# Keys, gates and key norms ahead of the exponentials, values by head pairs, and a new order of output-projection loads in a two-layer encoder trunk

## Time and profile before

| what | us |
|---|---|
| median of 3 runs | 1164.49 (1164.35 to 1165.43) |
| profiled execution, own time | 1163.36 |
| its span, first to last instruction | 1161.6 |
| PE busy | 1133.9 (98%) |
| DVE busy | 575.1 (50%) |
| ACT busy | 442.5 (38%) |
| POOL busy | 119.2 (10%) |

### The profile page before, as it was taken

The page is one execution under the profiler, slowest core; times in us unless marked ns, Lnnn a source line. Parts: engine busy times, 40 slices in busy tenths (PEclk is TensorE's granted clock), DMA queues, the critical chain, the costliest instruction groups (busy, mean ns, idle before and its releaser), DMA issues.

```text
span 1161.6 us, 13614 instructions
## 1 busy us (share of the span) xinstructions
PE 1133.9 (98%) x5059; PEld 903.0 (78%) x5059; DVE 575.1 (50%) x792; ACT 442.5 (38%) x685; POOL 119.2 (10%) x154
## 2 busy tenths in 40 slices
PE   7989999999999999999999989999999999999998
PEld 5767678888888888888877754578888888888887
DVE  6578875534434433241665686565443443442221
ACT  5545444423323322231546676544332233233120
POOL 5010200001101100000204210000010010010000
PEclk9999999999999999999999998999999999999999
DMA  6522123233233233222323210023223223223231
GB/s 187 191 66 62 54 78 104 87 94 108 87 94 108 87 94 107 92 92 90 91 75 93 74 37 19 1 73 109 91 91 108 90 90 108 90 91 101 81 125 56
DMA packets 84984, 103.88 MB, mean 89 GB/s; under 512 B 10579, under 2 KB 61456, under 8 KB 84816
## 3 DMA queue, kind: packets, MB, share of 16 engines
q1 hardware_dynamic: 81792, 101.99, 28.1%
q10 hardware_dynamic: 2096, 1.05, 0.3%
q0 software_dynamic: 1056, 0.30, 0.1%
HBM read 101.23 MB, written 2.10 MB: 89 GB/s over the span
## 4 chain that ended last, share of the span: by engine, by line
PE 91%; DVE 5%; ACT 2%; DMA 1%; issue 1%; POOL 0%; ACTq 0%; DVEq 0%; POOLq 0%
PE ps L1514 28%; PE ps L1516 28%; PE ps L1515 27%; PE ps L1889 2%; PE ps L1545 2%; PE ps L1915 2%; DMA x_tok<-in_x 1%; PE ps L1904 1%; DVE e_sc L1191 1%; ACT e_sc L740 1%; DVE e_sc L1180 1%; DVE tiny L1172 1%; PE ps L1891 0%; PE ps L1625 0%; PE ps L1964 0%
## 5 line engine op out<-in xcount | busy, mean ns | idle before, releaser
L1042 DVE TENSOR_TENSOR w_lo<-raw,w_hi 128x1024 fp32r<-128x1024 f32 (+2 forms) x194 | 228.1, 1180 | 446.7 <-ACT w_hi L652 443.7
L652 ACT ACTIVATE w_hi<-raw 128x1024 fp32r<-128x1024 f32 (+2 forms) x194 | 196.1, 1017 | 489.4 <-PE ps L1516 472.8
L1514 PE MATMUL ps<-h_hi,w_hi 128*128 128x512 f32 x928 | 367.6, 396 | 0.7 <-DVE conv_h L1211 0.7
L1516 PE MATMUL ps<-h_hi,w_lo 128*128 128x512 f32 x928 | 361.6, 390 | 0.0
L1515 PE MATMUL ps<-h_lo,w_hi 128*128 128x512 f32 x928 | 361.5, 390 | 0.0
L1514 PEld LDWEIGHTS ps<-h_hi,w_hi 128*128 128x128 f32 x928 | 174.4, 188 | 42.6 <-issue 5.7
L1515 PEld LDWEIGHTS ps<-h_lo,w_hi 128*128 128x128 f32 x928 | 174.5, 188 | 38.4 <-issue 2.6
L1516 PEld LDWEIGHTS ps<-h_hi,w_lo 128*128 128x128 f32 x928 | 174.3, 188 | 36.8
L545 POOL TENSOR_TENSOR ffn_t<-ffn_t,row_scale 128x512 f32<-128x512 f32 x40 | 50.9, 1293 | 555.0 <-ACT ffn_t L817 555.0
L1514 PE MATMUL ps<-w_hi,act_hi 128*128 128x512 f32 x176 | 68.7, 390 | 0.0
L1516 PE MATMUL ps<-w_hi,act_lo 128*128 128x512 f32 x176 | 68.5, 389 | 0.0
(11 more groups left out here) (254 smaller groups left out, 1249.6 us busy)
## 6 DMA issues: line engine op xcount, KB each, us to landing
raw<-in_w_ffn_in SPq DMA_DIRECT2D x88, 512.0 KB, 3.5
raw<-in_w_ffn_out SPq DMA_DIRECT2D x44, 512.0 KB, 3.7
raw<-in_e_w_in SPq DMA_DIRECT2D x18, 512.0 KB, 3.7
raw<-in_o_w_in SPq DMA_DIRECT2D x8, 512.0 KB, 3.6
raw<-in_o_w_out SPq DMA_DIRECT2D x8, 512.0 KB, 3.5
raw<-in_e_w_out SPq DMA_DIRECT2D x8, 256.0 KB, 3.9
raw<-in_e_w_out SPq DMA_DIRECT2D x4, 512.0 KB, 4.0
out_dram<-out_tok SPq DMA_DIRECT2D x8, 256.0 KB, 3.0
```

The source lines that it names most:

```text
L652: ins = act.activation(dst, src, ACT.Copy)
L1042: ins = TT(dst, src, high, ALU.subtract)
L1514: MM(dst, st_hi, mv_hi, start=start, stop=False)
L1516: return MM(dst, st_lo, mv_hi, start=False, stop=stop)
```

## The change

1. **Key tiles.** Both loads' key tiles come first (banks 4 to 7), then the gate matmuls, then all four key means into the banks of their own keys, then the values of both loads into banks 0, 1 and 3, 4. On ACT all key norms, a root table load ahead and an exponential table load behind them, lie before the first exponential; on DVE three of the four key norms do, and the fourth is behind the maxima of head 1.
2. **Values by head pairs.** `o_pT` and a second square buffer move into the space of `h_hi`, `o_pT` is doubled, and `o_values(j)` runs the matmuls of heads 2j and 2j+1 alternately into the two halves of bank 7. `o_out(j)` copies all 128 partitions at once.
3. **yc work spread.** The gate products and the sums of squares of `yc` are done two and two around heads 0 and 1. The splits of loads 116 and 117 move from before the head loop to its end (after head 6 and after the loop).
4. **Output projections.** Both take all four loads of the early operand first (`yb`; `yc`), then all four of the late one. The mean of the late operand comes after two loads; its bank is read before the fourth output tile of the third load is written. `residual` adds tiles 0 to 3 after the sixth load. The transposes of head 7 move inside the first load of the second projection and its values behind that load's second half.

```diff
-    k_pairs = (at("k_pair_a", ..., R + 45 * K), at("k_pair_b", ..., R + 72 * K))
+    k_pairs = (at("k_pair_a", ..., R + 45 * K), at("k_pair_b", ..., h_at + 16 * K))
-    o_pT = at("o_pT", [P, 3, S], F32, R + 58 * K)
+    o_pT = at("o_pT", [P, 2, 3, S], F32, h_at)
+    k_sq = at("k_sq", [P, 2, S], F32, h_at + 12 * K)
...
# ACT
+        key_squares(0)
+        key_squares(1)
+        rms_table()
         through(111)
-        kv_tiles(0)
-        through(112)
         rms(M_OK, ps[:, 4, :], 1)
         rms(M_OK + 1, ps[:, 5, :], 1)
-        kv_tiles(1)
-        through(113)
+        value_copy(0)
+        rms(M_OK + 2, ps[:, 6, :], 1)
+        rms(M_OK + 3, ps[:, 7, :], 1)
+        exp_table()
+        value_copy(1)
...
         o_exp(0)
-        rms(M_OK + 2, ps[:, 3, :], 1)
-        rms(M_OK + 3, ps[:, 7, :], 1)
+        o_exp(1)
         for h in range(HEADS):
-            if 1 <= h < 6:
+            if 1 <= h < HEADS - 1:
                 o_exp(h + 1)
-            if h >= 1:
-                o_out(h - 1)
+            if h and h % 2 == 0:
+                o_out(h // 2 - 1)
...
+            if h == 6:
+                rms_table()
+                through(112)
+        through(113)
+        o_out(3)
...
# DVE
+        key_gains(0)
+        key_gains(1)
+        through(111)
...
         k_norm(0)
-        through(112)
-        kv_tiles(1)
+        k_norm(1)
+        value_copy(0)
+        k_norm(2)
+        value_copy(1)
...
         o_max(0)
+        yc_gate(0)
+        yc_gate(1)
         o_prob(0)
         o_max(1)
-        k_norm(1)
-        through(113)
+        yc_gate(2)
+        yc_gate(3)
+        k_norm(3)
         for h in range(HEADS):
...
+            if h < 2:
+                yc_sum(2 * h)
+                yc_sum(2 * h + 1)
...
+            if h == 6:
+                through(112)
...
+        through(113)
         yd_sum(3)
...
         def residual(rnd, out0, bank0):
-            through(out0 + 3)
-            add_x(rnd, out0 + 3, 0, bank0)
+            through(out0 + 5)
+            add_x(rnd, out0 + 5, 0, bank0)
...
# PE
         pe.wait_ge(rs_step, M_EB + 1)
-        out_group(E_OUT, 4, (yb_hi, yb_lo), (ya_hi, ya_lo), (yb_lo_ready, ya_lo_ready), ea_mean)
-        pe.wait_ge(rs_step, M_EA + 1)
-        out_group(E_OUT + 4, 0, (yb_hi, yb_lo), (ya_hi, ya_lo), (yb_lo_ready, ya_lo_ready))
+        out_loads(E_OUT, 4, (yb_hi, yb_lo), yb_lo_ready, True, ea_mean)
+        out_loads(E_OUT + 2, 0, (yb_hi, yb_lo), yb_lo_ready, True, before=ea_read)
+        out_loads(E_OUT + 4, 4, (ya_hi, ya_lo), ya_lo_ready, False)
+        out_loads(E_OUT + 6, 0, (ya_hi, ya_lo), ya_lo_ready, False)
...
             for kt in range(QT):
-                pT = (o_pT[:, 0, :], o_pT[:, 1, 0:384], o_pT[:, 2, 0:256], o_pT[:, 1, 384:512])[kt]
-                ins = MM(ps[a:a + 64, 7, P * kt:S], o_v[:, kt, 64 * h:64 * h + 64], pT,
-                         start=kt == 0, stop=kt == QT - 1)
+                for i in range(2):
+                    a, h, p = 64 * i, 2 * j + i, o_pT[:, i]
+                    pT = (p[:, 0, :], p[:, 1, 0:384], p[:, 2, 0:256], p[:, 1, 384:512])[kt]
+                    ins = MM(ps[a:a + 64, 7, P * kt:S], o_v[:, kt, 64 * h:64 * h + 64], pT,
+                             start=kt == 0, stop=kt == QT - 1)
...
+        for h in range(HEADS - 1):
+            if 0 < h:
+                if h % 2 == 0:
+                    pe.wait_ge(rs_used, used_before(M_OK + h // 2))
+                else:
+                    pe.wait_ge(ok_normed, (h + 1) // 2 + 1)
                 o_scores(h + 1)
+            if h == 2:
                 pe.wait_ge(yc_summed, 4)
                 mean(M_OC, 3, ones, acc[:, :])
+                pe.wait_ge(rs_step, M_OK + 4)
+            if h and h % 2 == 0:
+                o_values(h // 2 - 1)
+            o_turn(h)
...
         pe.wait_ge(rs_step, M_OC + 1)
+        pe.wait_ge(d_exp_done, QT * HEADS)
+        out_loads(O_OUT, 0, (yc_hi, yc_lo), yc_lo_ready, True, od_tail)
+        out_loads(O_OUT + 2, 4, (yc_hi, yc_lo), yc_lo_ready, True, before=od_read)
+        out_loads(O_OUT + 4, 0, (yd_hi, yd_lo), yd_lo_ready, False)
+        out_loads(O_OUT + 6, 4, (yd_hi, yd_lo), yd_lo_ready, False)
```

More of the change, by code:

```diff
@@ L408, in _ @@
             for j in range(2):
-                n = E_OUT + 4 * half + j
+                n = E_OUT + 2 * half + j
                 free(n)
@@ L415, in _ @@
                                  .rearrange("(k p) n -> p k n", p=64)).then_inc(raw_landed[n % 2], 16)
+        for half in range(2):
             for j in range(2):
-                wide(E_OUT + 4 * half + 2 + j, e_w_out[0], 256 * j, 512 * half, 512)
+                wide(E_OUT + 4 + 2 * half + j, e_w_out[0], 256 * j, 512 * half, 512)
         def ffn(layer):
@@ L474, in _ @@
             wide(O_UKV + j, o_w_ukv[0], 0, 512 * j, 512)
-        for half in range(2):
-            for j in range(4):
-                wide(O_OUT + 4 * half + j, o_w_out[0], 256 * j, 512 * half, 512)
+        for part in range(2):
+            for half in range(2):
+                for j in range(2):
+                    wide(O_OUT + 4 * part + 2 * half + j, o_w_out[0], 512 * part + 256 * j, 512 * half, 512)
         ffn(1)
@@ L1519, in ready, with load @@
             pe.wait_ge(lo_done, n + 1 + shift)
-        def load(n, tiles, ks, moving, banks, first, last, shift=0, extra=None):
+        def load(n, tiles, ks, moving, banks, first, last, shift=0, extra=None, before=None):
             ready(n, shift)
@@ L1532, in load @@
                 for t, b in enumerate(banks):
+                    if before:
+                        before(kk, t)
                     ins = product(ps[0:P, b, :], th[t], tl[t], mh, ml,
@@ L1660, in _, with out_loads @@
         ab(3)
[L1662 to L1669, removed]
+        def out_loads(n, b0, tiles, lo_ready, first, extra=None, before=None):
+            th, tl = tiles
+            for j in range(2):
+                pe.wait_ge(lo_ready, 2 * j + 2)
+                load(n + j, plain(512, 4), (2 * j, 2 * j + 1), lambda k: (th[:, k, :], tl[:, k, :]),
+                     range(b0, b0 + 4), first and j == 0, not first and j == 1,
+                     extra=extra and (lambda: extra(j, 0)), before=before if j == 0 else None)
                 if extra:
@@ L1864, in k_means @@
-        def k_means(half):
-            for j in range(2):
-                p = 2 * half + j
-                pe.wait_ge(ok_gained, p + 1)
-                mean(M_OK + p, K_MEAN_BANKS[p], mean64, sq[:, j, :])
+            for kk in range(2):
+                for j in range(2):
+                    ins = product(ps[:, 4 + 2 * half + j, :], keys(w_hi, kk, j), keys(w_lo, kk, j),
+                                  ckv_hi[:, kk, :], ckv_lo[:, kk, :], kk == 0, kk == 1)
+            ins.then_inc(keys_done, 1)
@@ new lines, in value_tiles @@
+        def value_tiles(half):
+            n = O_UKV + half
+            values = lambda w, kk: w[:, n % W_SLOTS, 512 * kk + 256:512 * kk + 512]
+            if half == 0:
+                pe.wait_ge(gates_ready, 2)
+            else:
+                pe.wait_ge(gates_ready, 4)
+                pe.wait_ge(rs_step, M_OK + 1)
+            for t in range(QT):
+                for kk in range(2):
+                    c = 256 * (t % 2)
+                    ins = product(ps[:, V_BANKS[half][t // 2], c:c + 256], ckv_hi[:, kk, t * P:(t + 1) * P],
+                                  ckv_lo[:, kk, t * P:(t + 1) * P], values(w_hi, kk), values(w_lo, kk),
+                                  kk == 0, kk == 1)
+            ins.then_inc(load_used, 1)
@@ L1880, in _ @@
         ins.then_inc(gates_mixed, 1)
-        k_means(0)
-        kv_load(1)
+        for p in range(4):
+            pe.wait_ge(ok_gained, p + 1)
+            mean(M_OK + p, 4 + p, mean64, k_square(p))
+        value_tiles(0)
+        value_tiles(1)
         def o_scores(h):
```

210 lines of the change are left out of this document (90 added, 120 removed).

## The result

The changed kernel takes 1155.01 us (median of 4 runs, 1154.05 to 1156.05), and the kernel before, run beside it, 1164.42 us (median of 4 runs, 1163.84 to 1165.43): ratio 0.9915, 95% interval 0.9904 to 0.9927. That is 9.4 us less. The forecast was 1157.5 with a range of 1151.5 to 1162.5. The profiled execution took 1154.55 us with a span of 1152.7, 8.9 less than the span before.

What follows compares the result with a forecast made beforehand. PE, busy 98% of the span, bounds the kernel. Terms -3.5 - 8.8 + 5.1 + 0.9 = -6.3, a second count -7.9, about the middle -7.0: median 1157.5 us, range 1151.5 to 1162.5.

Steps and rivals of the forecast that it cites:

- First projection: First output projection: 2.2 us wait for ya's sum and 1.7 us of low clock go, 0.4 guard comes: -3.5 us.
- the guard: First projection, ahead of the third load's fourth output tile: PE waits 0.4 us for DVE's norm step.
- Values by pairs: Second attention: alternate array halves run side by side, 2.4 us per head pair instead of 4.6; four pairs -8.8 us.
- New waits: Second attention: PE waits walked through four streams total 13.2 us against 8.1 before, +5.1 us.
- The small waits of 0.3 and 0.6: Second attention, after head 1's wait: PE waits for head 2's exponentials and the last sum of yc.
- the guard for the mean of `yd`: Second output projection: PE waits 0.45 us, as in the first projection.
- Low clock: Second attention: old stretch goes (-3.3), 2.5 us come after head 1's wait and 1.7 after head 7's: +0.9 net.
- two sums: Whole change: adding the terms gives -6.3 us, counting the second stage out whole gives -7.9; about the middle, -7.0, taken.
- the first: Rival: clock stays up, or waits are shorter than walked (2 us less, no low clock 4.2): 1151.5 to 1155; chance 0.17.
- The copies as a bound: Rival, head loop: DVE and ACT become the bound, handoff slips in five heads give +5, 1162.5 us; chance 0.13.
- No overlap: Rival, pair values: halves do not run side by side since both write bank 7, +8.8, 1166.3 us; chance 0.04.
- A clock that stays down through the head loop: Rival, head 1's transposes to the first load: low clock lasts between waits, about +25, 1182 us; chance 0.03.

Runs made afterwards that it cites:

- The second experiment: Changed kernel, but the matmuls of a head pair's values run one head after the other, not alternating array halves: 1160.91 us, ratio 0.9962.
- The filler: Changed kernel plus 14 matmuls of 512 columns, result unread, in PE's wait before head 7's transposes: 1152.47 us, ratio 0.9899.
- The fifth experiment: Changed kernel with load 116's split behind the head loop, and the fourth key norm and yc's sums, squares, mean and norm re-placed: 1144.78 us, ratio 0.9832.

## Why the prediction was right, point by point

- **First projection, -3.5.** Measured -3.5 (48.53 to 44.99 us); 0.1 us of idle time is left for the guard where I had 0.4. `residual` with two loads between its halves delayed nothing: no wait before a feed-forward load stands in the list. Of the 3.5 us, the low clock's part depends on the execution: with the order put back the same wait was followed by full clock, and the stage cost 2.6.
- **Values by pairs, -8.8.** Measured 4 x (4.60 - 2.31) = -9.2: the perfect bound, where I had taken 2.4 per pair. The second experiment splits it into some 3 us for two heads in different halves behind one another and 6 for alternating.
- **New waits, 13.2 against 8.1.** The step was right in its places and 3.0 us too high in its size: 122.59 - 112.37 = 10.2 us idle. Head 1: 3.3 forecast, 3.3 measured. Head 7: 4.7 and 4.5. Exponentials of head 4: 1.9 and 1.4. Exponentials of head 0: 1.4 and 0.6. For the last I had the third key norm on DVE drawn out beside POOL (up to 1.4 us a step, as the earlier trace rows show once), but POOL's product ended at 679.8 and the step took 0.74. The small waits of 0.3 and 0.6 did not come, and the guard for the mean of `yd` cost 0.1 where I had 0.45.
- **Low clock, +0.9 net.** I had 4.2 us after and 3.3 before. Measured are two stretches of 3.4 us, half of which is 3.4 in all, against 3.4 before: no change. The length is not settled by the wait: behind head 1's wait of 3.3 us the stretch is 3.4 us in the changed kernel and 6.8 with the first projection put back. The filler shows that the wait before head 7 is the cause of its stretch. The waits of the nine profiles, from the first attention on, and what stood at their end: of 14 waits of 3.0 to 4.5 us each has half clock beginning within the wait or at most 1.3 us behind it; of 15 of 2.1 to 2.5 us nine have; of those of 1.2 to 1.6 us none. The rule of the Trainium skill that I weighed (TensorE: Matmul & The Clock Gate, "HAM oscillation — how this bites in real kernels") says that bursts of matmuls broken by waits fall back to the low clock again and again, and the trace agrees for the long waits. But the waits that it tells of are of 3 to 5 us, so the third low stretch that I drew from it for a wait of 1.9 us was my reading and not the section's; the 1.4 us wait of head 4 was followed by full clock. The row that I held against it was luck in its turn: the wait of 2.4 us, harmless in the kernel before, has low clock at its end in five of the other eight profiles.
- **Sum.** -7.0 forecast, -9.4 measured by the medians. The forecast was the middle of two sums that count the second stage as -2.8 and -4.4 us; that stage measured -6.6. The difference is in the terms above: waits 3.0 too high, clock 0.9, values 0.4. (The list of new waits adds up to 13.05 and not 13.2, and the matmuls of the second sum to 107.6 and not 107.4; neither matters.) Taken off -2.8 they give -7.1, so 0.5 us stay unexplained. So the mechanism was right, and one term, the waits, was too high by 3.0 us, a third of the gain, with two smaller errors to the same side; the result lies 2.5 us below the forecast and inside the range.
- **Rivals.** Of the first, the half on shorter waits came true and the half on the clock did not; the result lies at its upper end, 1155. The copies as a bound fell by the second and fifth experiments: longer values cost nearly their full length, and the stage from the gates on runs 9.7 us faster with the same copies. (The Trainium skill, TensorEngine Tiling (Array Packing), "PSUM Bottleneck", names such a bound; these runs do not show it.) No overlap fell by the 2.31 us of a pair. A clock that stays down through the head loop did not come in any of the eight profiles with the new loop; the longest low stretch is 6.8 us.

What the change left on the table is its own wait before head 7: the split of load 116 was not moved far enough back, and it and its low clock took back 5.1 us; the order around head 1 and the norm of `yc` took another 5.1 by the medians, 4.3 by the stage.

## What to carry to other kernels

When matmuls with half-width outputs stand in one stream, alternate the two halves: 2.31 us for two heads here, 3.86 one after the other. Where streams are hand-ordered, walk each one with the durations of the old trace before moving work: work that nobody needs yet must not stand before a step that the busiest engine waits for. The fifth experiment gained by placing it where that engine has a long step. Count a long wait of TensorE (3 us and more here) at its length plus the low clock behind it: 1.6 us here before head 7, and up to twice that where the stretch was 6.8 us long. Where single executions differ by a low stretch, compare stages and not spans.

## What the runs showed of the hardware

- Two series of half-width matmuls in different halves overlap by 0.7 us even when they are issued one after the other (3.86 instead of 4.60 us, in four of four pairs); alternated, they overlap fully (2.31 us) though both write one bank.
- A wait of 2.4 us was followed by the 2.4 GHz level in one execution and by the 1.2 GHz level in another, with the same work on both sides. All 14 waits of 3.0 us or more had the lower level at their end, for 3.4 or 6.8 us.
- 14 matmuls without use made the kernel faster, by 1.6 us in the stage.
